# Joint 512-column matmuls in three of the seven Strassen products of a decoder block's feed-forward stages

## The reference

```python
def swiglu(x, w_gate, w_up, w_down):
    return (jax.nn.silu(x @ w_gate) * (x @ w_up)) @ w_down
...
x = layer_norm(DN_ALPHA * x + 0.5 * swiglu(x, ffn1_w_gate[i], ffn1_w_up[i], ffn1_w_down[i]), ln_g[i, 0], ln_b[i, 0])
```

## Time and profile before

| | |
|---|---|
| median of 3 runs | 2185.89 us (2184.53 to 2186.52) |
| span of the profiled execution | 2184.3 us |
| PE busy | 2161.4 us (99%), 13640 matmuls |
| weight loads busy | 1918.4 us (88%) |
| DVE busy | 1334.5 us (61%) |
| ACT busy | 1068.6 us (49%) |
| POOL busy | 779.0 us (36%) |
| HBM | 94 GB/s over the span |

### The profile page before, as it was taken

How to read it: one execution, slowest core, us unless ns; L and a number is a source line. 1 busy time by engine, 2 the same in 40 slices (tenths; PEclk the granted TensorE clock), 3 DMA queues, 4 the chain that set the end, 5 groups by cost and what they waited for, 6 DMA issues and landing times.

```text
span 2184.3 us, 35402 instructions
## 1 busy us (share of the span) xinstructions
PE 2161.4 (99%) x13640; PEld 1918.4 (88%) x13640; DVE 1334.5 (61%) x2315; ACT 1068.6 (49%) x1927; POOL 779.0 (36%) x573
## 2 busy tenths in 40 slices
PE   9999999999999999999999999999999999999998
PEld 8999998878888989898899999887778887989896
DVE  7656667464436928385766666657655346747475
ACT  4434345563435525254643534466654445535353
POOL 3201116567638030305420111555548555120203
PEclk9999999999999999999999999999999999999999
DMA  4323334213313333333232333320004312333332
GB/s 152 122 93 95 110 113 134 77 49 109 123 39 107 107 97 108 95 110 123 87 118 96 97 107 114 119 79 29 20 11 132 110 49 77 116 97 96 108 97 78
DMA packets 58199, 207.50 MB, mean 95 GB/s; under 512 B 6960, under 2 KB 7088, under 8 KB 57264
## 3 DMA queue, kind: packets, MB, share of 16 engines
q1 hardware_dynamic: 56016, 197.68, 28.9%
q10 hardware_dynamic: 2016, 7.55, 0.9%
HBM read 203.10 MB, written 2.10 MB: 94 GB/s over the span
## 4 chain that ended last, share of the span: by engine, by line
PE 93%; DVE 3%; ACT 1%; POOL 1%; issue 1%; DMA 0%; DVEq 0%; ACTq 0%
PE bank L1772 14%; PE bank L1773 14%; PE bank L1774 14%; PE bank L1983 11%; PE bank L1988 11%; PE bank L1985 11%; PE bank L2184 2%; PE bank L2145 2%; PE bank L2117 1%; PE bank L2118 1%; PE bank L1872 1%; PE bank L1874 1%; PE bank L1873 1%; PE bank L1791 1%; PE bank L1802 1%
## 5 line engine op out<-in xcount | busy, mean ns | idle before, releaser
L627 POOL TENSOR_TENSOR w_lo<-w_raw,w_hi 128x1024 fp32r<-128x1024 f32 (+1 forms) x226 | 530.1, 2354 | 1175.3 <-ACT w_hi L804 1175.2
L1772 PE MATMUL bank<-h_hi,w_hi 128*128 128x512 f32 x960 | 377.8, 394 | 1.5 <-DVE h_lo L1751 0.8
L1773 PE MATMUL bank<-h_lo,w_hi 128*128 128x512 f32 x960 | 374.4, 390 | 0.0
L1774 PE MATMUL bank<-h_hi,w_lo 128*128 128x512 f32 x960 | 373.8, 389 | 0.0
L804 ACT ACTIVATE w_hi<-w_raw 128x1024 fp32r<-128x1024 f32 (+1 forms) x227 | 230.4, 1021 | 130.5 <-PE bank L1774 92.4
L1772 PEld LDWEIGHTS bank<-h_hi,w_hi 128*128 128x128 f32 x960 | 180.3, 188 | 45.5 <-issue 3.3
L1774 PEld LDWEIGHTS bank<-h_hi,w_lo 128*128 128x128 f32 x960 | 180.2, 188 | 38.2
L1773 PEld LDWEIGHTS bank<-h_lo,w_hi 128*128 128x128 f32 x960 | 180.5, 188 | 34.2
L1983 PE MATMUL bank<-x_hi,w_hi 128*128 128x256 f32 x864 | 139.6, 284 | 0.3
L1772 PE MATMUL bank<-x_hi,w_hi 128*128 128x512 f32 x352 | 139.2, 396 | 0.0
L1988 PE MATMUL bank<-x_hi,w_lo 128*128 128x256 f32 x864 | 138.9, 283 | 0.0
(11 more groups left out here) (307 smaller groups left out, 5036.0 us busy)
## 6 DMA issues: line engine op xcount, KB each, us to landing
w_raw<-w_dram SPq DMA_DIRECT2D x315, 512.0 KB, 3.5
w_raw<-w_dram SPq DMA_DIRECT2D x64, 448.0 KB, 3.3
f<-mem_dram ACTq DMA_DIRECT2D x5, 1024.0 KB, 5.2
out_dram<-t SPq DMA_DIRECT2D x8, 256.0 KB, 2.2
t<-x_dram SPq DMA_DIRECT2D x2, 512.0 KB, 6.9
f<-cmp_w_dram ACTq DMA_DIRECT2D x1, 1024.0 KB, 4.9
t<-x_dram ACTq DMA_DIRECT2D x2, 256.0 KB, 5.5
t<-x_dram ACTq DMA_DIRECT2D x1, 512.0 KB, 8.1
```

Of the source, the lines that this page charges most:

```text
L627: pool.tensor_tensor(w_lo[:, slot(s), 0:n * P], w_raw[:, s % RAW, 0:n * P], w_hi[:, slot(s), 0:n * P].bitcast(F32), ALU.subtract).then_inc ...
L1772: pe.matmul(dst, w_hi[:, slot(s), w], m_hi[:, k, :], start=k == 0, stop=False)
L1773: pe.matmul(dst, w_hi[:, slot(s), w], m_lo[:, k, :], start=False, stop=False)
L1774: last = pe.matmul(dst, w_lo[:, slot(s), w], m_hi[:, k, :], start=False, stop=k == n - 1)
```

## The change

Three products become `quarter_joint`: prod6, prod5 and prod3. The hi by hi and w_hi by x_lo matmuls of one weight block are one matmul of 512 columns. Its moving operand is 256 columns of the rounded half and 256 of the remainder (for that, x_hi and x_lo become one tensor `x`, and the combined rows in `ra` get a view of both halves); its result fills both halves of bank_a. The four w_lo matmuls stay and add to the left half. So twelve matmuls and weight loads become eight.

The running sum now lies in two halves that someone has to add. ACT's keep2 and keep3 copy the right half instead of the left, and DVE adds the left half from the bank to the copy in new operations `join2` and `join3`. After prod3, ACT copies the right half (`right_last`), DVE adds the left (`join_last`), and ACT then applies SiLU in SBUF. prod5 waits for `joined2` instead of `snap2`, prod3 for `joined3` instead of `snap3`.

Besides, three semaphores are folded into others: the three iotas now count on `pool_set`, the negated sinks on `dist_ready`, and `up1_out` and `up2_out` are one `up_out`.

```diff
-                    act.activation(snaps(g, 1), bank_a(g)[:, 0:256], ACT.Copy).then_inc(snap2, 1)
+                    act.activation(snaps(g, 1), bank_a(g)[:, 256:512], ACT.Copy).then_inc(snap2, 1)
...
-                    act.activation(snaps(g, 2), bank_a(g)[:, 0:256], ACT.Copy).then_inc(snap3, 1)
+                    act.activation(snaps(g, 2), bank_a(g)[:, 256:512], ACT.Copy).then_inc(snap3, 1)
...
-                def silu_second(g):
+                def right_last(g):
                     act.wait_ge(m3, g.count + 1)
                     act.wait_ge(z["hidden"], st.p0 + g.pair - 1)
-                    act.activation(gated[g.pair % 2][:, half[1]], bank_a(g)[:, 0:256], ACT.Silu).then_inc(z["gated"], 1)
+                    act.activation(gated[g.pair % 2][:, half[1]], bank_a(g)[:, 256:512], ACT.Copy).then_inc(last_right, 1)
+
+                def silu_second(g):
+                    act.wait_ge(last_out, g.count + 1)
+                    own = gated[g.pair % 2][:, half[1]]
+                    act.activation(own, own, ACT.Silu).then_inc(z["gated"], 1)
...
+                def join2(g):
+                    dve.wait_ge(snap2, g.count + 1)
+                    dve.tensor_tensor(snaps(g, 1), snaps(g, 1), bank_a(g)[:, 0:256], ALU.add).then_inc(joined2, 1)
+
+                def join3(g):
                     dve.wait_ge(snap3, g.count + 1)
+                    dve.tensor_tensor(snaps(g, 2), snaps(g, 2), bank_a(g)[:, 0:256], ALU.add).then_inc(joined3, 1)
+
+                def join_last(g):
+                    own = gated[g.pair % 2][:, half[1]]
+                    dve.wait_ge(last_right, g.count + 1)
+                    dve.tensor_tensor(own, own, bank_a(g)[:, 0:256], ALU.add).then_inc(last_out, 1)
...
+                        if before:
+                            join_last(before)
+                        if g.next:
                             if g is not begin:
                                 gate_rest(g.next)
+                        join2(g)
+                        if g.next:
                             pair_rest(g.next)
...
                         if g.next:
                             up_rest(g.next)
+                        join3(g)
                         before = g
...
+            def quarter_joint(g, w, i, both, begin, rest, done):
+
+                hi, lo = w
+                a = bank_a(g)[:].rearrange("p (h s) -> p h s", h=2)
+                columns = [slice(512 * i + P * k, 512 * i + P * k + P) for k in range(4)]
+                for k, c in enumerate(columns):
+                    pe.matmul(a, hi[:, c], both[:, :, k, :], start=begin and k == 0, stop=False, skip_group_check=True)
+                pe.wait_ge(*rest)
+                for k, c in enumerate(columns):
+                    last = pe.matmul(a[:, 0, :], lo[:, c], both[:, 0, k, :], start=False, stop=k == 3, skip_group_check=True)
+                last.then_inc(done, 1)
```

More of the change, by code:

```diff
@@ L310, in build @@
         t = sb("t", [P, KC, SEQ])
-        x_hi = sb("x_hi", [P, KC, SEQ], F32R)
-        x_lo = sb("x_lo", [P, KC, SEQ], F32R)
+        x = sb("x", [P, 2, KC, SEQ], F32R)
+        x_hi, x_lo = x[:, 0], x[:, 1]
         with nc.sbuf_tensor("ta", [P, KC, SEQ], F32) as ta:
@@ L374, in build @@
                 4: (t4[0], t4[1])}
+        rows_joint = ra[:, 0:2048].rearrange("p (h k s) -> p h k s", h=2, k=4)
         lng = sb("lng", [P, NLN, KC])
@@ L457, in build @@
         snap1, snap2, snap3 = [sem(f"snap{i}") for i in range(1, 4)]
-        first_out, up2_out, up1_out = sem("first_out"), sem("up2_out"), sem("up1_out")
+        first_out, last_right, last_out, up_out = sem("first_out"), sem("last_right"), sem("last_out"), sem("up_out")
+        joined2, joined3 = sem("joined2"), sem("joined3")
         diff_ready, comb_hi, comb_lo = sem("diff_ready"), sem("comb_hi"), sem("comb_lo")
@@ L634, in _ @@
             pool.memset(eps[:], EPS).then_inc(pool_set, 1)
[L635 removed]
+            pool.iota(dist_i[:, 0:512], [[1, 512]], base=-384, channel_multiplier=-1).then_inc(pool_set, 1)
             pool.iota(dist_i[:, 512:640].rearrange("p (i n) -> p i n", i=NT), [[-128, NT], [16, 32]], base=0,
[L637 to L639 removed]
+                      channel_multiplier=-1).then_inc(pool_set, 1)
+            pool.iota(dist_i[:, 640:896], [[1, 256]], base=-128, channel_multiplier=-1).then_inc(pool_set, 1)
+            pool.wait_ge(pool_set, 8)
             pool.affine_select(out=ident[:], in_=ident[:], compare_op=ALU.not_equal, fill=1.0, base=0,
@@ L710, in mixer @@
                     pool.wait_ge(x_ready, KC * (st.ln + 1))
-                    pool.wait_ge(sinks_neg, 1)
+                    pool.wait_ge(dist_ready, 6)
                     for p in range(2):
@@ L943, in ffn @@
                         if before:
+                            right_last(before)
                             silu_second(before)
@@ L1250, in _ @@
         def _(dve):
-            dve.wait_ge(iota_done, 3)
+            dve.wait_ge(pool_set, 8)
             dve.tensor_copy(dist[:, 0:512], dist_i[:, 0:512]).then_inc(dist_f, 1)
@@ L1487, in up2, with up1 @@
                 def up2(g):
-                    dve.wait_ge(snap3, g.count + 1)
-                    dve.wait_ge(m7, g.count + 1)
-                    dve.tensor_tensor(bank_b(g)[:, half[1]], snaps(g, 2), bank_b(g)[:, half[0]], ALU.add).then_inc(up2_out, 1)
-                def up1(g):
-                    dve.wait_ge(snap2, g.count + 1)
-                    dve.wait_ge(m4, g.count + 1)
-                    dve.tensor_tensor(bank_b(g)[:, half[0]], snaps(g, 1), bank_b(g)[:, half[0]], ALU.add).then_inc(up1_out, 1)
-                    dve.wait_ge(up1_out, g.count + 1)
-                    hid(g.pair, bank_b(g)[:], -0.5)
+                    dve.wait_ge(joined3, g.count + 1)
+                    dve.wait_ge(m7, g.count + 1)
+                    dve.tensor_tensor(bank_b(g)[:, half[1]], snaps(g, 2), bank_b(g)[:, half[0]], ALU.add).then_inc(up_out, 1)
+                def up1(g):
+                    dve.wait_ge(joined2, g.count + 1)
+                    dve.wait_ge(m4, g.count + 1)
+                    dve.tensor_tensor(bank_b(g)[:, half[0]], snaps(g, 1), bank_b(g)[:, half[0]], ALU.add).then_inc(up_out, 1)
+                    dve.wait_ge(up_out, 2 * g.count + 2)
+                    hid(g.pair, bank_b(g)[:], -0.5)
+                def join2(g):
+                    dve.wait_ge(snap2, g.count + 1)
+                    dve.tensor_tensor(snaps(g, 1), snaps(g, 1), bank_a(g)[:, 0:256], ALU.add).then_inc(joined2, 1)
+                def join3(g):
+                    dve.wait_ge(snap3, g.count + 1)
+                    dve.tensor_tensor(snaps(g, 2), snaps(g, 2), bank_a(g)[:, 0:256], ALU.add).then_inc(joined3, 1)
[3 more added lines that the diff above has]
+                    dve.tensor_tensor(own, own, bank_a(g)[:, 0:256], ALU.add).then_inc(last_out, 1)
                 begin = st.groups[0][0]
@@ L1638, in mixer @@
                 if st.kind == "swa":
-                    dve.wait_ge(sinks_neg, 1)
+                    dve.wait_ge(dist_ready, 6)
                 def recip(u):
@@ L1964, in shift @@
             def shift(st):
-                pe.wait_ge(pool_set, 6)
+                pe.wait_ge(pool_set, 9)
                 pe.wait_ge(lead_ready, st.ln + 1)
@@ L2011, in prod3 @@
                 def prod3(g):
-                    pe.wait_ge(snap3, g.count + 1)
+                    pe.wait_ge(joined3, g.count + 1)
                     pe.wait_ge(pair_hi, 2 * g.count + 2)
-                    quarter(bank_a(g)[:, 0:256], w_pair(g, 1), 1, x_block(1, 1), False, (late_lo, g.count + 1), m3)
+                    quarter_joint(g, w_pair(g, 1), 1, x[:, :, 4:8, half[1]], False, (late_lo, g.count + 1), m3)
                 def prod4(g):
@@ L2019, in prod4 @@
                     pe.wait_ge(up_hi, g.count + 1)
[L2020 removed]
+                    pe.wait_ge(up_out, 2 * g.count + 1)
                     quarter(bank_b(g)[:, half[0]], w_up(g), 0, comb[4], False, (up_lo, g.count + 1), m4)
```

15 lines of the change are left out of this document (4 added, 11 removed).

## The result

The changed kernel took 2221.39 us, the median of four runs (2219.33 to 2225.71), against 2185.21 before: a ratio of 1.0164, interval 1.015 to 1.0179. It is slower by 36 us. The forecast was 2215 us.

A forecast was written before the change was run, and what follows sets the result against it. PE bounded the kernel before, DVE having 1.2 us to spare per group; afterwards the DVE-ACT ring would. Parts of seven added 11.8 us, parts of five 16.8, refilling 0.4, giving 2213.3 profiled and 2215 us as the time; its own range 2208 to 2222.

The forecast's parts named there:

- two causes: join2 queued behind DVE's weight sums before a part's first prod5, and the ring of DVE and ACT in later groups.
- The ring: DVE and ACT wait on each other through join_last, SiLU, keep2 and pair_rest: 10.31 us per group against PE's 9.92.
- The waits at the start: First prod5: 3.65 us per stage, 0.71 per part of seven; prod3: 0.88 first in a stage, 0.34 in seven's second group.
- The waits of the ring: PE waits at prod3 for joined3, 0.39 us in each group once the ring is the limit.
- PE's saving: A joint product takes 1.386 us instead of 1.44, 0.054 saved; 228 products give 12.3 us.
- Refilling: Refilling PE's pipeline after waits, 0.4 us added for the whole kernel.
- 2.61 of waits: PE's waits in one part of seven groups: 0.71 + 0.34 + 1.56 us, before subtracting the joint products' saving.
- Rival C: PE's clock falls in the new 3.65 us gaps at stage starts: +8 to +16 us, about 2227; 10%.
- 11.8 + 16.8 + 0.4: Added us: eight parts of seven groups, four parts of five groups, and refilling PE's pipeline.
- A: The adds on DVE are hidden and only PE's saving counts: 2174 us; 3%.
- B: Weight loads on PE are the limit, 912 fewer save 128 us: 2057 us; 1%.
- D: Only the stage starts cost, the ring never closes: +9 us, 2195; 10%.

The follow-up runs named there:

- silu_behind: Changed kernel with the SiLU after join_last moved behind keep2 and the first pair rounding in ACT's queue; 2205.26 us.
- join2_early: Changed kernel with join2 of each part's first group moved earlier in DVE's queue (ahead of the weight sums at stage starts, of gate_rest elsewhere); 2206.61 us.
- early_and_behind: Changed kernel with both reorderings, those of silu_behind and join2_early; 2192.62 us.
- wait_only: Kernel before plus one wait: prod5 of each stage's first group also waits for the fourth weight sum; no joins or joint matmuls; 2202.25 us.
- hybrid: full_copy in the two parts of seven groups of each stage, the part of five as in the kernel before; 2179.37 us.
- joint_only: Kernel before with the joint matmuls alone in prod6, prod5 and prod3; right half neither copied nor added, so result incomplete; 2179.40 us.
- split_adds: Changed kernel with its copies, adds and waits, but each joint matmul split into two of 256 columns; 2222.96 us.
- joint_flat: joint_only with 512 contiguous moving columns instead of two pieces of 256, computing from other columns; 2178.47 us.
- joint_flat_out: joint_flat with the output also written as one row of 512 columns; 2175.71 us in one run.
- full_copy: silu_behind with keep2 and keep3 copying the whole bank, prod5 and prod3 waiting only for that copy, and DVE adding the halves in SBUF; 2186.02 us.

## Why the prediction was right

**Direction and mechanism: right.** Its two causes are there, each taken away alone (silu_behind, join2_early) and both together (early_and_behind), and the gap also made alone (wait_only).

**The ring: right.** 10.31 us forecast, 10.31 measured from `up2` to `up2`. This is not luck, for its pieces agree as well: 3.20 from `up2` to `join_last` (163.12 to 166.32) for 3.19, 2.12 from `join_last` to `pair_rest` (166.32 to 168.44) for 2.12, and 0.45 from `join3` to `up2` (162.67 to 163.12) for 0.45. In silu_behind, where ACT no longer closes the ring, the groups average 9.98 us. The working had 9.98 for DVE's own work, but PE's own 9.96 is too near to tell the two apart.

**The waits at the start: right in place and size.** First prod5 of a stage 3.65 forecast, 3.69 to 3.73 measured; first prod5 of a part of seven 0.71 and 0.70; prod3 of a part of seven's second group 0.34 and 0.30; first prod3 of a stage 0.88 and 0.90, in the one stage in which the clock didn't fall; in the other three it was nothing. The waits of the ring are 0.24 to 0.27 and not 0.39, for the two next reasons.

**PE's saving: the term was too large.** "0.054 saved" per joint product was 0.04; 0.93 for four lies between the two bounds, 0.906 (4 x 0.2265) and 0.96 (4 x 0.24). In the ring it costs nothing, since PE waits; in the groups without a ring it costs 0.04 each.

**Refilling: the term was too small.** I added "0.4 for the refilling" in all. Every wait makes the product that waited 0.07 to 0.12 us longer, 0.10 in the mean, nearly all of it between its first matmul and its second (0.335 us apart in the prod3 that waited, 0.233 without a wait). A ring wait of 0.25 plus 0.10 plus 0.04 for the slower joint matmuls makes up the 0.39. In front of the ring nothing absorbs it: a part of seven has 0.12 after its first prod5, 0.04 in the second group and 0.09 in the third more than forecast, in all 0.25. The forecast's 2.61 of waits less 20 joint products (the 21st stands behind the stretch measured here) was +1.53 by this measure; +1.79 was measured. Eight parts: 2 us.

**Clock: a rival that came true in part.** Rival C, given 10%, had the clock fall in the gaps. It fell at three of four in the profiled run and cost 2.5 us, where C had 8 to 16: the low stretches lasted 3.4, 6.8 and 3.4 us and not about 8, and, as C's own text said, prod3's wait covers some of it. The other three runs had mean granted clocks of 0.992, 0.994 and 0.990 against 0.994, and times of 2222.37, 2220.41 and 2225.71: the lower the clock, the longer the run. That this is why the median lies 2 us above the profiled run fits, but the other runs have no trace to show it.

**The sum.** Forecast 11.8 + 16.8 + 0.4 = 29.0. Measured in the parts: 8 x 1.79 = 14.3 and 20.4 (213.6 less 193.2), of which 2.5 is the clock. With 1.5 us back elsewhere the span grew by 33.2, and the median by 36. The forecast missed by 6.4 us: 4.2 in the span (some 5.4 in the parts from the three small terms above, which all lay on the same side, less the 1.2 before the first group), and 2.1 by which the median lies above the profiled run. The measured time is at the upper edge of the forecast's own range (2208 to 2222), and not for the reason that the range was drawn for: the adds were no dearer than the rows said (0.33 to the next operation, 0.45 to one that depends on it).

**Rivals A, B and D: wrong.** A needed hidden adds: it took another order of ACT's queue, another copy and the part of five left alone (hybrid) before they were hidden. B: 912 weight loads less brought 7.4 us in joint_only, not 128. Its 0.141 us for a load is the busy time shared out over the loads, which overlap; one lasts 0.19. The Trainium skill, "Perfetto Trace Analysis", section "Identifying the Most-Contended Engine", would have TensorE judged by the busy share of its weight loads, beside its share of peak arithmetic. The first was 88% in the earlier trace rows and is 85% now, and here it doesn't tell what fewer loads bring, since loads that last 0.19 us each follow one another at 0.12. D, the ring that never closes, is silu_behind, and the rows of the changed kernel show the ring closed in 52 groups. D's price of 2195 us was 10 too low even for that kernel (2205): it has the same three terms too small, and the clock fell at all four gaps there.

## What to carry to other kernels

An add that is cheap by its duration is dear by its place: ask of each new small operation what stands ahead of it in its engine's queue and who is held behind it, and when two in-order queues wait for each other once per turn, add up the turn; it may be longer than the busy time of any engine in it. Let the engine that is fast release the buffer (here ACT copying all of it) and the busy one do its sum later from the copy. And put such a change only where the busy engine has room: stage starts, where it is late already, may have to stay as they are.

## What the runs showed of the hardware

- **The clock fell at waits of 2.5 to 3.7 us, but not at all of them.** At such waits of PE the granted clock went to 0.50 (1.2 GHz) in 3 of 4 cases in the changed kernel, in 4 of 4 in wait_only, silu_behind and early_and_behind (here at waits of 2.5 us), in 2 of 4 in split_adds, and in 1 of 4 in join2_early (again 2.5 us). It fell between 1.5 us before PE's next matmul and 1.5 us after it, and stayed low for 3.4 to 6.8 us. What decides between them no run shows. In wait_only, where nothing covered it, a fall cost 1.3 to 1.4 us and 2.4 in the longest case; in the changed kernel, where a wait stood behind it, 0.55 and 1.44.
- **It also fell where no wait had been added:** for 3.4 us once between 1453 and 1487 us, far from any group, in split_adds, early_and_behind, hybrid and joint_flat, of which the last two have none of these waits.
- **A wait of PE costs more than its length:** 0.06 to 0.12 us in the product behind it, in every case from 0.13 us of waiting up (a low clock apart).
- **Joint matmuls of 512 columns between short ones start 0.2325 us apart**, plain ones of 512 in runs of their own 0.2265; the shape of the operands is not the reason (joint_flat_out), and the reason is open.
- **An add of 256 columns costs DVE the same with one operand in a bank as with both in SBUF:** 0.41 to 0.43 us in both, with the next operation 0.33 us later (full_copy and hybrid against the changed kernel).
